# The opening of a two-model kernel: decay's second low-rank product behind the first value chunk, ScalarE's splits and read-outs ahead of mixes, the key factor spread inside r's first chunk

## The chip, the cores and the metric

The kernel runs on one core of a Trainium2 chip. Its time is the device time of one execution in microseconds (us): 1493.51 us as the median of three runs (1492.37 to 1494.57). The core has five engines that follow their own instruction streams and meet at semaphores: TensorE (PE; its weight loads are listed as PEld), VectorE (DVE), ScalarE (ACT), GpSimd (POOL) and SyncE (SP), which here only issues DMAs.

## The reference

Two small models run one after the other on one sequence of 256 tokens with 1024 features. All that the change touches lies in the first 115 us, in the opening of the first layer, an RWKV-7 time mix:

```
x_prev = jnp.pad(h[:, :-1], ((0, 0), (1, 0), (0, 0)))
xx = x_prev - h
xs = h[None] + xx[None] * mu[:, None, None, :]
x_r, x_w, x_k, x_v, x_a, x_g = xs[0], xs[1], xs[2], xs[3], xs[4], xs[5]
rkv = jnp.einsum('pbtd,pde->pbte', jnp.stack([x_r, x_k, x_v]), w_rkv)
w = -jax.nn.softplus(-(w0 + jnp.tanh(x_w @ w1) @ w2)) - 0.5
decay = jnp.exp(-jnp.exp(w.astype(f32)))
a = jax.nn.sigmoid(a0 + (x_a @ a1) @ a2)
g = jax.nn.sigmoid(x_g @ g1) @ g2
kk = to_heads((k * k_k).astype(f32))
kk = kk / jnp.maximum(jnp.linalg.norm(kk, axis=-1, keepdims=True), 1e-12)
k = k * (1.0 + (a - 1.0) * k_a)
...
_, y = lax.scan(step, S0, (tm(r_h), tm(w_h), tm(k_h), tm(v_h), tm(kk), tm(b_h)))
```

Six mixes of each token with the one before feed three large products (k, v, r, each 1024 x 1024) and three low-rank pairs: decay (64), rate a (64) and gate (160). The keys are normalised for each of 16 heads. The scan over tokens then needs all of it. Behind it come the layer's output, an MLP, attention, and the second model, which the change leaves as they are.

## The kernel before, in words

**Large products.** A weight matrix comes in units of 128 x 2048 floats (1 MB). SP loads a unit into one of four `raw` buffers, ScalarE rounds it to `whi` (`hi_unit`, L418, two buffers), VectorE takes the remainder `wlo = raw - whi` (`lo_unit`, L874, two buffers), and TensorE makes three passes for each product: hi x hi, hi x lo, lo x hi (`passes`, L1631 to L1633). The inputs are split likewise into `XH` and `XL`. A chunk is two units: 512 output columns in two PSUM banks. The chunks of the opening are k0, k1 (units 0 to 3), v0, v1 (4 to 7) and r0, r1 (8 to 11). Chunks take the banks 0, 1 and 2, 3 in turn. The split of unit u needs unit u - 2 to be used up (`unit_used`), and its load needs unit u - 4 to be split (`lo_done`).

**What sets the order.** Each engine's stream is written out by hand and runs strictly in that order; `hi_upto(n)` and `lo_upto(n)` put the splits of all units below n at that place. A wait of one instruction holds everything behind it on its engine.

**The opening's side work.** The input is normalised and turned into `hT`. VectorE makes the mixes: `mix(1)` for w, `mix(2)` for v, `mix(3)` for a, `mix(4)` for r, `mix(5)` for g (L1085, eight instructions each); those that feed large products are split by ScalarE (`mix_to_hi`, L608) and VectorE (`mix_to_lo`, L1095). ScalarE also copies chunks out of PSUM (`read_chunk`: k by L487, v by L491).

- `decay_and_rate` (L1830): first products of decay and rate, after k1. ScalarE's tanh and copy follow (L617).
- `gate_in` (L1838, L1840): first products of the gate, after v0, into banks 6 and 7; ScalarE's sigmoids follow (L624, L626).
- `head_sums` (L1748): sums of squared keys per head, bank 0; VectorE reads them (`head_means`, L1021), ScalarE takes the root (`head_roots`, L565), VectorE inverts (`head_inverses`, L1028, L1029), TensorE spreads the factor to all features (`head_spread`, L1764), VectorE multiplies (L1157).
- The second low-rank products (L1866) first for decay, then for rate, in banks 4 to 7, between `head_sums` and v1; ScalarE's sigmoids follow (L634), then for decay a scaling to `lwT` (L641). VectorE's running sum over tokens (the scan, L1142) waits for it, and `centred` (L1150) closes that block.
- `gates` (L1880, L1884): second products of the gate, in the middle of r0.
- At the end VectorE makes the scan's operands (L1167 to L1172, the semaphore `prepared`), and TensorE's `prepare(0)` (L1911, L1920) starts the blockwise inverse, whose first step on VectorE is L1189.

Of the kernel before, what the change touches and what calls it, by code (L numbers as in the profile page):

```python
# [166 lines left out]
def build(nc, a, out):  # L167

    with ExitStack() as ctx:
# [191 lines left out]
        def _(sp):  # L361
# [26 lines left out]
            for name, kt, nn in GEMMS:  # L388
                if kt:
                    for i in range(nn * kt // UK):  # L390
# [20 lines left out]
        def _(act):  # L411
# [217 lines left out]

            for q, (dst, bias) in enumerate(((sT, "w0"), (aT, "a0"))):  # L630
# [6 lines left out]
                if q == 0:  # L637

                    act.wait_ge(lora2_read, 4)
                    act.wait_ge(mix_lo, 2)  # L640
                    act.activation(lwT, sT, ACT.Copy, scale=-float(np.exp(-0.5))).then_inc(lw_ready, 1)  # L641
# [1667 lines left out]
```

## Time and profile before

| what | us |
|---|---|
| median of three runs | 1493.51 (1492.37 to 1494.57) |
| the profiled execution's own time | 1492.59 |
| its span, first to last instruction | 1490.7 |
| TensorE busy | 1413.4 (95%) |
| VectorE busy | 938.7 (63%) |
| ScalarE busy | 704.6 (47%) |
| GpSimd busy | 69.2 (5%) |
| mean granted TensorE clock | 0.986 of full |

The span leaves out some 1.9 us around the first and the last instruction. A busy share is a mean over stages with different limits; TensorE is busy 95% of the whole, but less in the opening, and for a change there only the opening's rows count.

### The profile page before, as it was taken

The numbers are of one execution on the slowest core, as the hardware profiler recorded it, in microseconds if no ns is written. First come the engines' busy times: TensorE is split into PE (matmuls) and PEld (weight loads), VectorE is DVE, ScalarE is ACT, GpSimd is POOL, SyncE is SP. The second block draws the span as 40 slices with busy tenths as digits, with TensorE's granted clock in tenths as the row PEclk, the third lists the DMA queues.
The fourth block names the chain that finished last, engine by engine and source line by source line (L and its number), as shares of the span: only waits on it lengthen the run. The fifth ranks groups of instructions, "written<-read, shape, count | busy, mean of one in ns | idle before, by whom it ended". The sixth has DMA issues, their size and how long they took to land.

```text
span 1490.7 us, 22267 instructions
## 1 busy us (share of the span) xinstructions
PE 1413.4 (95%) x9462; PEld 1213.4 (81%) x9462; DVE 938.7 (63%) x1286; ACT 704.6 (47%) x998; POOL 69.2 (5%) x62
## 2 busy tenths in 40 slices
PE   5889988999999989999999999999999999899998
PEld 5769887888889957888889887778888897688887
DVE  6677675565666586656667643566566577575565
ACT  5473332454445555545444444445444525455443
POOL 0005260000001000000000000000000000000000
PEclk9999999999999999999999999999999999999999
DMA  8320002455555421555575553345555543345552
GB/s 312 111 102 3 30 3 81 168 179 195 198 184 204 170 87 40 187 193 183 191 242 173 198 190 124 136 150 190 197 185 185 202 145 138 113 142 197 192 183 78
DMA packets 35284, 230.42 MB, mean 155 GB/s; under 512 B 4192, under 2 KB 5536, under 8 KB 8560
## 3 DMA queue, kind: packets, MB, share of 16 engines
q1 hardware_dynamic: 33376, 223.43, 43.4%
q0 software_dynamic: 1808, 5.56, 1.2%
q8 instruction: 75, 1.23, 0.3%
q14 instruction: 25, 0.20, 0.0%
HBM read 227.90 MB, written 1.05 MB: 154 GB/s over the span
## 4 chain that ended last, share of the span: by engine, by line
PE 83%; DVE 10%; ACT 5%; issue 2%; DMA 0%; SPq 0%; DVEq 0%; POOL 0%; ACTq 0%
PE bank L1631 16%; PE bank L1632 16%; PE bank L1633 16%; PE bank L1707 15%; PE bank L1710 8%; DVE wlo L874 3%; ACT whi L418 2%; PE bank L1950 2%; PE bank L1593 1%; DVE arena L1085 1%; DVE arena L1204 1%; PE bank L1967 1%; DVE arena L1360 1%; DVE arena L1339 1%; ACT arena L576 1%
## 5 line engine op out<-in xcount | busy, mean ns | idle before, releaser
L874 DVE TENSOR_TENSOR wlo<-raw,whi 128x2048 fp32r<-128x2048 f32 x208 | 478.1, 2299 | 395.4 <-ACT whi L418 395.0
L418 ACT ACTIVATE whi<-raw 128x2048 fp32r<-128x2048 f32 x208 | 398.4, 1916 | 411.8 <-PE bank L1633 276.7
L1631 PE MATMUL bank<-whi,XHL 128*128 128x512 f32 x896 | 352.6, 394 | 11.6 <-DVE XHL L921 7.5
L1632 PE MATMUL bank<-wlo,XHL 128*128 128x512 f32 x896 | 349.9, 391 | 0.0
L1633 PE MATMUL bank<-whi,XHL 128*128 128x512 f32 x896 | 349.6, 390 | 0.0
L1707 PE MATMUL bank<-XHL,whi 128*128 128x512 f32 x1024 | 323.4, 397 | 2.3 <-DVE arena L949 2.2
L1710 PEld LDWEIGHTS bank<-XHL,wlo 128*128 128x128 f32 x1024 | 192.9, 188 | 45.5
L1631 PEld LDWEIGHTS bank<-whi,XHL 128*128 128x128 f32 x896 | 168.7, 188 | 50.6 <-issue 8.1
L1710 PE MATMUL bank<-XHL,wlo 128*128 128x256 f32 x1024 | 201.7, 278 | 0.0
L1633 PEld LDWEIGHTS bank<-whi,XHL 128*128 128x128 f32 x896 | 168.9, 188 | 35.9
L1632 PEld LDWEIGHTS bank<-wlo,XHL 128*128 128x128 f32 x896 | 169.0, 189 | 33.2
L1707 PEld LDWEIGHTS bank<-XHL,whi 128*128 128x128 f32 x1024 | 158.5, 190 | 5.8 <-DVE arena L949 3.0
L1631 PE MATMUL bank<-XHL,whi 128*128 128x256 f32 x512 | 149.3, 292 | 9.1 <-DVE XHL L1100 5.0
L1632 PE MATMUL bank<-XHL,whi 128*128 128x256 f32 x512 | 147.4, 288 | 0.0
L1633 PE MATMUL bank<-XHL,wlo 128*128 128x256 f32 x512 | 147.2, 287 | 0.0
L1631 PEld LDWEIGHTS bank<-XHL,whi 128*128 128x128 f32 x512 | 100.9, 197 | 11.7 <-issue 8.0
L1632 PEld LDWEIGHTS bank<-XHL,whi 128*128 128x128 f32 x512 | 101.1, 197 | 0.1
L1633 PEld LDWEIGHTS bank<-XHL,wlo 128*128 128x128 f32 x512 | 100.9, 197 | 0.0
L508 ACT ACTIVATE arena<-bank 128x256 f32<-128x256 f32 x128 | 47.8, 374 | 49.6 <-PE bank L1710 49.6
L513 ACT ACTIVATE XHL<-arena 128x256 fp32r<-128x256 f32 x128 | 46.1, 410 | 53.1 <-DVE arena L952 53.1
L952 DVE SCALAR_TENSOR_TENSOR arena<-arena 128x256 f32<-128x256 f32 x128 | 54.4, 425 | 4.4
L949 DVE TENSOR_TENSOR arena<-bank,arena 128x256 f32<-128x256 f32 x128 | 53.5, 418 | 0.0
(280 smaller groups left out, 1201.9 us busy)
## 6 DMA issues: line engine op xcount, KB each, us to landing
raw<-in_w_mlp SPq DMA_DIRECT2D x128, 1024.0 KB, 4.8
raw<-in_w_rv SPq DMA_DIRECT2D x8, 1024.0 KB, 5.0
raw<-in_w_rg SPq DMA_DIRECT2D x8, 1024.0 KB, 4.9
raw<-in_w_reo SPq DMA_DIRECT2D x8, 1024.0 KB, 4.8
raw<-in_w_k SPq DMA_DIRECT2D x4, 1024.0 KB, 9.3
raw<-in_w_v SPq DMA_DIRECT2D x4, 1024.0 KB, 5.7
raw<-in_w_r SPq DMA_DIRECT2D x4, 1024.0 KB, 4.8
raw<-in_w_rwo SPq DMA_DIRECT2D x4, 1024.0 KB, 5.0
```

The costliest lines, as they stand in the source:

```text
L418: act.activation(whi[:, u % SPLIT_RING], raw[:, u % RAW_RING], ACT.Copy).then_inc(hi_done, 1)
L508: act.activation(UPL[:, t % 4], psum[up_bank(t)][:, T:2 * T], ACT.Copy).then_inc(up_low, 1)
L513: act.activation(XH[:, KT + t % 8], HID[:, t % 4], ACT.Copy).then_inc(h_hi, 1)
L874: dve.tensor_tensor(wlo[:, u % SPLIT_RING], raw[:, u % RAW_RING], whi[:, u % SPLIT_RING].bitcast(F32), ALU.subtract).then_inc(lo_done, 1)
L949: dve.tensor_tensor(UPZ[:, t % 2], psum[up_bank(t)][:, 0:T], UPL[:, t % 4], ALU.add)\
L952: dve.scalar_tensor_tensor(HID[:, t % 4], UPZ[:, t % 2], 0.0, UPZ[:, t % 2], ALU.max, ALU.mult)\
L1631: pe.matmul(out_, xh[xs], wh[ws], start=start, stop=False)
L1632: pe.matmul(out_, xh[xs], wl[ws], start=False, stop=False)
L1633: return pe.matmul(out_, xl[xs], wh[ws], start=False, stop=stop_)
L1707: pe.matmul(bank[:, :], whi[:, u % SPLIT_RING, k2 + e, cols], XHL[:, kt + e].rearrange("p h t -> p (h t)"), start=(kt + e == 0), stop=False)
L1710: ins = pe.matmul(bank[:, 0:T], wlo[:, u % SPLIT_RING, k2 + e, cols], XH[:, kt + e], start=False, stop=(kt + e == KT - 1))
L1950: ins = pe.matmul(psum[bank][rows, p * HD:(p + 1) * HD], w[rows, f, p], x[rows, f, p], start=(p == 0), stop=(p == KT - 1))
```

## The change

It moves work on four engines, and adds or removes no arithmetic.

- **Loads.** The weight units 2 and 3 (k1's) are issued ahead of the gate's matrix g1 and all that follows it, and no longer behind the constants.
- **ScalarE and VectorE at the start.** The first pair of turned features is handled ahead of the split of unit 0.
- **Around k1.** ScalarE reads k0 and splits unit 3 ahead of splitting the mix for v; VectorE splits unit 3 ahead of it too. ScalarE splits unit 5 right behind reading k1.
- **Behind v0.** TensorE makes decay's second product first, then `gate_in` (now in banks 0 and 1), `head_sums` (now in bank 2), rate's second product. v1 now also waits until VectorE has read bank 2 (`sums_ms`), and r0 until ScalarE has read banks 0 and 1 (`lora1_act`). ScalarE does decay's sigmoids before the keys' squares and the split of unit 7, and the gate's sigmoids after rate's.
- **VectorE behind v0.** `head_means` comes ahead of the split of unit 7, and the split of unit 8 ahead of `head_inverses`.
- **r0.** `head_spread` moves from ahead of r0 to behind its second of eight feature tiles.

```diff
             load_unit("k", 0, 0)
             load_unit("k", 1, 1)
-            for n, dst in (("w1", w1s), ("a1", a1s), ("g1", g1s)):
+            for n, dst in (("w1", w1s), ("a1", a1s)):
                 sp.dma_start(dst.rearrange("p k n -> p (k n)"), a[n]).then_inc(lora_in, 16)
+            load_unit("k", 2, 2)
+            load_unit("k", 3, 3)
+            sp.dma_start(g1s.rearrange("p k n -> p (k n)"), a["g1"]).then_inc(lora_in, 16)
...
             norm_first()
-            hi_upto(1)
             for b in range(4):
+                if b == 1:
+                    hi_upto(1)
                 act.wait_ge(turned, b + 1)
...
             hi_upto(3)
+            read_chunk("k", 0, by_feature(kT))
+            hi_upto(4)
             mix_to_hi(2, 1)
-            read_chunk("k", 0, by_feature(kT))
             read_chunk("k", 1, by_feature(kT))
+            hi_upto(6)
             act.wait_ge(lora1, 2)
...
             mix_to_hi(4, 0)
             read_chunk("v", 0, by_token_plain(V))
-            act.wait_ge(prepared, 1)
-            head_squares(0, KKR)
-            act.wait_ge(lora1, 3)
-            act.activation(sga, psum[6][:, 0:T], ACT.Sigmoid).then_inc(lora1_act, 1)
...
-            hi_upto(U0["v"] + 4)
...
+            act.wait_ge(mixed, 5)
+            low_rank_out(0, sT, "w0")
+            act.wait_ge(prepared, 1)
+            head_squares(0, KKR)
+            hi_upto(U0["v"] + 4)
+            act.wait_ge(lora1, 3)
+            act.wait_ge(lora2_read, 4)
+            act.wait_ge(mix_lo, 2)
+            act.activation(lwT, sT, ACT.Copy, scale=-float(np.exp(-0.5))).then_inc(lw_ready, 1)
+            low_rank_out(1, aT, "a0")
+            act.activation(sga, psum[0][:, 0:T], ACT.Sigmoid).then_inc(lora1_act, 1)
...
+            hi_upto(U0["r"] + 1)
             head_roots(0)
-            hi_upto(U0["r"] + 1)
...
             mix(2, 3)
+            lo_upto(4)
             mix_to_lo(1, 2, 1)
-            lo_upto(4)
             mix(3, 4)
...
-            lo_upto(8)
             dve.wait_ge(lora2, 4)
             head_means(0, 1.0, 0.0)
+            lo_upto(8)
...
+            lo_upto(9)
             head_inverses(0)
-            lo_upto(9)
...
             chunk("v", 0, "token", 1, ready=lambda b: pe.wait_ge(mix_lo, 1))
-            pe.wait_ge(mixed, 5)
-            gate_in()
-            pe.wait_ge(acc_read["act"], READ_COUNT[CHUNK0["v"]][1])
-            pe.wait_ge(const_in, 16 * (len(CONST_KEEP) - 2))
-            head_sums(0, KKSQ)
...
+            low_rank(0, w2s, tw)
+            pe.wait_ge(mixed, 5)
+            pe.wait_ge(acc_read["act"], READ_COUNT[CHUNK0["v"]][1])
+            gate_in()
+            pe.wait_ge(const_in, 16 * (len(CONST_KEEP) - 2))
+            head_sums(0, KKSQ)
+            low_rank(1, a2s, ta)
+            pe.wait_ge(sums_ms, 1)
             chunk("v", 1, "token", 1)
 
-            pe.wait_ge(lora2_read, 8)
-            head_spread(0, rn)
+            def key_spread():
+
+                pe.wait_ge(lora2_read, 8)
+                head_spread(0, rn)
...
-            chunk("r", 0, "feature", 0, ready=lambda b: pe.wait_ge(mix_lo, 2), mid=(4, gates))
+            pe.wait_ge(lora1_act, 4)
+            chunk("r", 0, "feature", 0, ready=lambda b: pe.wait_ge(mix_lo, 2), mids=((2, key_spread), (4, gates)))
```

ScalarE around k1, before (L418 splits a unit, L608 the mix for v, L487 reads a k chunk):

```order
L418 ACTIVATE whi<-raw 128x2048 [waits unit_used,raw_landed2]
L608 ACTIVATE XHL<-arena 128x8x256 [waits mixed]
L487 ACTIVATE arena<-bank 128x512 [waits unit_used]
L487 ACTIVATE arena<-bank 128x512
L418 ACTIVATE whi<-raw 128x2048 [waits unit_used,raw_landed3]
```

and now, where the same lines are L421, L490 and L612:

```order
L421 ACTIVATE whi<-raw 128x2048 [waits unit_used,raw_landed2]
L490 ACTIVATE arena<-bank 128x512 [waits unit_used]
L490 ACTIVATE arena<-bank 128x512
L421 ACTIVATE whi<-raw 128x2048 [waits unit_used,raw_landed3]
L612 ACTIVATE XHL<-arena 128x8x256 [waits mixed]
```

The split of unit 3 has moved ahead of the wait for the mix.

TensorE between v0 and v1, before (L1838 and L1840 are `gate_in`, L1748 `head_sums`, L1866 the second products of decay and then of rate):

```order
L1838 MATMUL bank6<-arena 128x256 [waits mixed]
L1838 MATMUL bank6<-arena 128x256 x7
L1840 MATMUL bank7<-arena 32x256 x8
L1748 MATMUL bank0<-arena,c_head_window 32x256 [waits sq_ready,const_in,acc_read_act]
L1748 MATMUL bank0<-arena,c_head_window 32x256 x7
L1866 MATMUL bank4<-arena 128x256 [waits lora1_act]
...
L1866 MATMUL bank6<-arena 128x256 [waits lora1_act]
...
L1866 MATMUL bank4<-arena 128x256 [waits lora2_read]
...
L1866 MATMUL bank6<-arena 128x256 [waits lora2_read]
```

and now (L1875 are the second products, L1851 and L1853 `gate_in`, L1761 `head_sums`):

```order
L1875 MATMUL bank4<-arena 128x256 [waits lora1_act]
...
L1875 MATMUL bank6<-arena 128x256 [waits lora1_act]
...
L1851 MATMUL bank0<-arena 128x256 [waits acc_read_act,mixed]
L1851 MATMUL bank0<-arena 128x256 x7
L1853 MATMUL bank1<-arena 32x256 x8
L1761 MATMUL bank2<-arena,c_head_window 32x256 [waits sq_ready,const_in]
L1761 MATMUL bank2<-arena,c_head_window 32x256 x7
L1875 MATMUL bank4<-arena 128x256 [waits lora2_read]
...
L1875 MATMUL bank6<-arena 128x256 [waits lora2_read]
```

Decay's product now stands ahead of the gate's, and rate's behind the head sums.

VectorE behind the keys' product with their factor, before (L874 splits a unit, L1021 is `head_means`, L1142 the scan, L1150 its centring, L1028 and L1029 `head_inverses`, L1157 the product with the spread factor):

```order
L874 TENSOR_TENSOR wlo<-raw,whi 128x2048 [waits hi_done]
L1021 TENSOR_SCALAR arena<-bank0 128x256 [waits sums_ready,lora2]
L1138 MEMSET arena 128x16 [waits lw_ready,mix_lo]
...
L1150 TENSOR_TENSOR arena<-arena,small 128x2064 [waits dve_step]
L1028 TENSOR_SCALAR arena<-arena 128x256 [waits sums_sd]
L1029 RECIPROCAL arena<-arena 128x256 [waits dve_step]
L874 TENSOR_TENSOR wlo<-raw,whi 128x2048 [waits hi_done]
L1157 TENSOR_TENSOR arena<-arena,bank4 128x2x256 [waits rn_spread,lora2]
```

and now (L883, L1030, L1148, L1160, L1037, L1038, L1167 in the same roles):

```order
L1030 TENSOR_SCALAR arena<-bank2 128x256 [waits sums_ready,lora2]
L883 TENSOR_TENSOR wlo<-raw,whi 128x2048 [waits hi_done]
L1148 MEMSET arena 128x16 [waits lw_ready,mix_lo]
...
L1160 TENSOR_TENSOR arena<-arena,small 128x2064 [waits dve_step]
L883 TENSOR_TENSOR wlo<-raw,whi 128x2048 [waits hi_done]
L1037 TENSOR_SCALAR arena<-arena 128x256 [waits sums_sd]
L1038 RECIPROCAL arena<-arena 128x256 [waits dve_step]
L1167 TENSOR_TENSOR arena<-arena,bank4 128x2x256 [waits rn_spread,lora2]
```

Both splits have changed places with their neighbour of the key norm.

## Rows read from the trace of the kernel before

**Rows 1.** The page: the chain that ended last, by engine

```profile
PE 83%; DVE 10%; ACT 5%; issue 2%; DMA 0%; SPq 0%; DVEq 0%; POOL 0%; ACTq 0%
```

**Rows 2.** Busy time by stretch: us, PE, PEld, DVE, ACT, POOL, clock, DMA share, GB/s

```profile
0.00:113.70 113.70, 87.77 (x544) 73.44 (x544) 79.40 (x128) 64.68 (x85) 1.23 (x6) 0.94 0.50 172
25.20:40.10 14.90, 14.83 (x123) 14.63 (x122) 12.89 (x20) 5.96 (x5) 0.00 (x0) 1.00 0.63 232
43.10:49.10 6.00, 5.97 (x28) 5.97 (x29) 6.00 (x11) 0.00 (x0) 0.00 (x0) 0.50 0.50 175
61.10:63.20 2.10, 0.04 (x2) 0.02 (x1) 2.10 (x2) 1.91 (x1) 0.00 (x0) 1.00 0.00 0
196.00:198.00 2.00, 1.78 (x34) 1.78 (x36) 1.38 (x3) 0.31 (x1) 1.29 (x1) 0.50 0.00 0
```

**Rows 3.** Timeline of TensorE where k1's and v0's second units start: start, length, [idle before]

```profile
43.13 0.58 PE L1631 MATMUL bank<-XHL,whi 128*128 128x256 f32 x1 [3.10 <-DVE wlo L874]
...
63.18 0.50 PE L1631 MATMUL bank<-whi,XHL 128*128 128x512 f32 x1 [2.06 <-DVE wlo L874]
```

**Rows 4.** Timeline of ScalarE, 35 to 61 us

```profile
36.06 1.92 ACT L608 ACTIVATE XHL<-arena 128x2048 fp32r<-128x2048 f32 x1 [5.53 <-DVE arena L1085]
37.88 1.07 ACT L487 ACTIVATE arena<-bank 128x512 f32<-128x512 f32 x2
38.83 3.71 ACT L418 ACTIVATE whi<-raw 128x2048 fp32r<-128x2048 f32 x2
...
58.90 1.90 ACT L418 ACTIVATE whi<-raw 128x2048 fp32r<-128x2048 f32 x1
```

**Rows 5.** Timeline of VectorE, 37 to 47 us

```profile
38.01 2.29 DVE L1095 TENSOR_TENSOR XHL<-arena,XHL 128x2048 fp32r<-128x2048 f32 x1 [1.99 <-ACT XHL L608]
40.78 2.29 DVE L874 TENSOR_TENSOR wlo<-raw,whi 128x2048 fp32r<-128x2048 f32 x1 [0.48 <-ACT whi L418]
```

**Rows 6.** Timeline of TensorE from v0's end to v1's start

```profile
68.77 3.62 PE L1838 MATMUL bank<-arena 128*128 128x256 f32 x16
...
77.89 2.00 PE L1866 MATMUL bank<-arena 64*128 64x256 f32 x16 [1.07 <-ACT arena L626]
81.28 1.14 PE L1866 MATMUL bank<-arena 64*128 64x256 f32 x8 [1.39 <-ACT arena L634]
...
83.81 0.50 PE L1631 MATMUL bank<-whi,XHL 128*128 128x512 f32 x1
```

**Rows 7.** Timeline of ScalarE, 79 to 85 us

```profile
79.68 3.01 ACT L634 ACTIVATE arena<-bank,vecs 128x256 f32<-128x256 f32 x8
82.72 1.91 ACT L641 ACTIVATE arena<-arena 128x2048 f32<-128x2048 f32 x1
```

**Rows 8.** Timeline of VectorE, 79 to 117 us

```profile
84.78 0.07 DVE L1138 MEMSET arena<- 128x16 f32 x1 [2.35 <-ACT arena L641]
...
97.19 2.47 DVE L1157 TENSOR_TENSOR arena<-arena,bank 128x512 f32<-128x512 f32 x4
99.82 2.29 DVE L874 TENSOR_TENSOR wlo<-raw,whi 128x2048 fp32r<-128x2048 f32 x1 [0.16 <-ACT whi L418]
102.03 2.19 DVE L1167 TENSOR_SCALAR arena<-arena,vecs 128x256 f32<-128x256 f32 x8
...
113.19 2.28 DVE L874 TENSOR_TENSOR wlo<-raw,whi 128x2048 fp32r<-128x2048 f32 x1
115.39 1.28 DVE L1189 TENSOR_TENSOR arena<-bank,c_scan_masks 128x512 f32<-128x512 f32 x2
```

**Rows 9.** Timeline of TensorE from v1's end to the blockwise inverse

```profile
95.23 1.15 PE L1764 MATMUL bank<-arena 32*128 32x256 f32 x16 [0.21 <-issue]
97.38 0.35 PE L1631 MATMUL bank<-XHL,whi 128*128 128x256 f32 x1 [1.00 <-issue]
...
107.80 0.39 PE L1631 MATMUL bank<-XHL,whi 128*128 128x256 f32 x1
...
113.74 2.09 PE L1911 MATMUL bank<-arena 64*64 64x64 f32 x128
```

**Rows 10.** Busy time by stretch, around the end of k0

```profile
32.00:34.00 2.00, 2.00 (x19) 2.00 (x19) 2.00 (x5) 0.00 (x0) 0.00 (x0) 1.00 0.36 53
```

More of the change, by code:

```diff
@@ L620, in _, with low_rank_out @@
             read_chunk("v", 0, by_token_plain(V))
-            act.wait_ge(prepared, 1)
-            head_squares(0, KKR)
-            act.wait_ge(lora1, 3)
-            act.activation(sga, psum[6][:, 0:T], ACT.Sigmoid).then_inc(lora1_act, 1)
-            for b in range(4):
-                ins = act.activation(sgb[b * QUARTER:(b + 1) * QUARTER, :], psum[7][0:QUARTER, 0:T], ACT.Sigmoid)
-            ins.then_inc(lora1_act, 1)
-            hi_upto(U0["v"] + 4)
-            for q, (dst, bias) in enumerate(((sT, "w0"), (aT, "a0"))):
+            def low_rank_out(q, dst, bias):
                 for b in range(4):
@@ L636, in _ @@
                     ins.then_inc(lora2_read, 1)
[L637 to L641, printed above, removed]
+            act.wait_ge(mixed, 5)
[9 more added lines that the diff above has]
+            act.activation(sga, psum[0][:, 0:T], ACT.Sigmoid).then_inc(lora1_act, 1)
+            for b in range(4):
+                ins = act.activation(sgb[b * QUARTER:(b + 1) * QUARTER, :], psum[1][0:QUARTER, 0:T], ACT.Sigmoid)
+            ins.then_inc(lora1_act, 1)
+            hi_upto(U0["r"] + 1)
             head_roots(0)
-            hi_upto(U0["r"] + 1)
             act.wait_ge(centred, 1)
@@ L1017, in head_means @@
             def head_means(i, scale, eps):
-                r, bank = (rn, 0) if i == 0 else (frn, 4)
+                r, bank = (rn, 2) if i == 0 else (frn, 4)
                 dve.wait_ge(sums_ready, i + 1)
@@ L1078, in _ @@
             norm_first()
-            lo_upto(1)
             def mix_tiles(order, mu, ks):
@@ L1108, in _ @@
                 mix_tiles(0, 2, range(2 * b, 2 * b + 2)).then_inc(first_mixed, 1)
-                if b >= 1:
+                if b == 0:
+                    lo_upto(1)
+                else:
                     first_to_lo(b - 1)
@@ L1633, in passes, with chunk @@
                 return pe.matmul(out_, xl[xs], wh[ws], start=False, stop=stop_)
-            def chunk(name, n, form, half=0, kts=KT, ready=None, mid=None, by_rows=False):
+            def chunk(name, n, form, half=0, kts=KT, ready=None, mid=None, by_rows=False, mids=()):
                 g = CHUNK0[name] + n
@@ L1652, in chunk @@
                             mid[1]()
+                        for first_kt, work in mids:
+                            if kt == first_kt:
+                                work()
                         if by_rows and kg == kts // UK - 1:
@@ L1747, in head_sums @@
                     q, j = p // 4, p % 4
-                    ins = pe.matmul(psum[4 if i else 0][32 * j:32 * j + 32, 0:T], keep["head_window"][:, 14 - 2 * q:46 - 2 * q],
+                    ins = pe.matmul(psum[4 if i else 2][32 * j:32 * j + 32, 0:T], keep["head_window"][:, 14 - 2 * q:46 - 2 * q],
                                     sq[:, p], start=(q == 0), stop=(q == 1 and i == 0))
@@ L1837, in gate_in @@
                 for k in range(KT):
-                    pe.matmul(psum[6][:, 0:T], g1s[:, k, 0:P], XM[1][:, k], start=(k == 0), stop=(k == KT - 1))
+                    pe.matmul(psum[0][:, 0:T], g1s[:, k, 0:P], XM[1][:, k], start=(k == 0), stop=(k == KT - 1))
                 for k in range(KT):
-                    ins = pe.matmul(psum[7][0:QUARTER, 0:T], g1s[:, k, P:GATE], XM[1][:, k], start=(k == 0),
+                    ins = pe.matmul(psum[1][0:QUARTER, 0:T], g1s[:, k, P:GATE], XM[1][:, k], start=(k == 0),
                                     stop=(k == KT - 1))
@@ L1849, in _, with low_rank @@
             chunk("v", 0, "token", 1, ready=lambda b: pe.wait_ge(mix_lo, 1))
[L1850 to L1856 removed]
+            def low_rank(q, w2, t1):
                 for half in range(2):
                     if q == 0:
[L1859 removed]
+                        pe.wait_ge(lora1_act, 2)
                     else:
```

4 lines of the change are left out of this document (1 added, 3 removed).

## The prediction, written before the changed kernel ran

> **What bounds the kernel now.** I read the chain of waits first: 83% of it is TensorE, 10% VectorE, 5% ScalarE [rows 1], so time that TensorE does not spend idle or at the slow clock is time won. The table of stretches then says where such time lies in the part that changes: up to 113.7 us TensorE is busy 87.8 us, and its clock averages 0.94 [rows 2]. The timeline of TensorE in that part names the waits, and those of ScalarE and VectorE say what they wait behind. Last I looked at who is late once those waits are gone. There VectorE shows: from 84.78 to 115.39 it runs with one gap of 0.16 us [rows 8]. It will be the new limit, so TensorE's gain is not the answer by itself.
>
> **Part 1, k1's second unit.** TensorE waits 3.10 us for VectorE's split of unit 3 [rows 3]. ScalarE did the mix at 36.06, read k0, and only at 38.83 began units 3 and 4 [rows 4]; VectorE then split unit 3 from 40.78 to 43.07 [rows 5]. A unit of TensorE takes 5.7 us (v1's two run from 83.81 to 95.23 less 0.21 of idle [rows 6, 9]); with TensorE done with unit 2 at 43.13 - 3.10 = 40.03, k0 was done at 34.3. So now: k0 read 34.3 to 35.35 (1.07), unit 3 rounded to 37.2 (3.71 for two, so 1.86), VectorE, free since its mix ended at 36.06, done at 39.5 (2.29). TensorE asks at 40.0: the wait of 3.10 goes, with 0.5 us to spare. With it goes its aftermath: the clock is 0.50 (1.2 GHz) from 43.1 to 49.1, after an idle of 3.10 us, and 1.00 before [rows 2]. Six us at half speed hold 3.0 us of work, so 3.0 us more are lost; I take 2.85, because 5.97 of the 6.00 was work and the edges are blurred. Sum of part 1: 5.95 us. The mix for v now ends its two splits at 38.9 and 41.7, and v0 wants it at 49.
>
> The Trainium skill, TensorE: Matmul & The Clock Gate, section "HAM oscillation — how this bites in real kernels", says that an idle gap throttles the array again and the slow start is paid anew. The trace agrees at 43.1, and at 61.1 to 63.2, where 2.06 us of idle left the clock at 1.00 [rows 2, 3].
>
> The loads cannot spoil this. The same bytes go out in another order, and at 32 to 34 us the DMA share is down to 0.36 [rows 10], so the whole list including v's first units is nearly drained when k1 starts at 34.3. The start itself (pair 0 ahead of unit 0's split on both engines) only swaps neighbours on one chain; I count 0 to 0.3 us and take 0.
>
> **Part 2, v0's second unit.** The wait of 2.06 us [rows 3] came from ScalarE rounding unit 5 at 58.90 [rows 4], behind tanh and the next mix. Now it stands right behind reading k1, done near 48.7, and VectorE's part near 52.5; TensorE, 5.95 us early, asks at 55.1. The 2.06 goes: 8.0 us ahead at v0's end, 60.75 for 68.77.
>
> **Part 3, between v0 and v1.** Before: 68.77 to 83.81 = 15.04 us with waits of 1.07, 1.39 and 0.32 (81.28 + 1.14 to 82.74) [rows 6]. Now the same products follow each other: decay 2.0 (operands ready at 51.5), gate and head sums 77.89 - 1.07 - 68.77 = 8.05, rate 2.0. Their waits are over: v0 is read at 61.9 while decay's product runs to 62.75, the keys' squares are ready at 68.1, decay's sigmoids (3.01, [rows 7]) end at 66.2. Sum 12.05, v1 starts at 72.8, 11.0 ahead. The added wait for VectorE's read of bank 2 needs head sums (70.8) plus 0.42: 71.3, under rate's product. If it were late, v1 and all behind it would queue.
>
> **Part 4, VectorE's chain.** Its start is decay's `lwT`, which overwrites what `gate_in` reads. ScalarE is free at 69.9 (sigmoids to 66.2, squares to 68.1, unit 7 to 69.9), the gate's first products end at 69.5; 1.91 more [rows 7] gives 71.85. VectorE reads bank 2 at 70.9 to 71.3 and splits unit 7 to 73.5, so its scan starts at 73.55 where it started at 84.78 [rows 8]: 11.2 ahead. From there the same instructions follow, but for one wait. Before, the product with the spread factor started 12.41 after the scan's start (84.78 to 97.19) with no idle. Now this work ends at 73.55 + 12.41 - 0.05 = 85.9 to 86.1, and TensorE spreads only after two tiles of r0. v1 ends at 72.8 + 11.3 = 84.1, half a unit is 2.9, half of the spread (1.15, [rows 9]) gives the first bank at about 87.9. VectorE idles 1.85 us; the old 0.16 goes. So L1189, at 115.39 before, comes 11.2 - 1.85 + 0.16 = 9.5 us earlier, at 105.9.
>
> **Part 5, TensorE up to there.** Before, v1's end to the inverse was 95.23 to 113.74 = 18.5 us with 0.21 and 1.00 of waiting [rows 9]; now 17.3, ending at 101.4, 12.3 ahead. But the rest waits for VectorE: operands at 101.6, r0's read by ScalarE is tied to the last of them (103.75, then 1.07), r1's first tiles to VectorE's split that ends at 105.9 (113.19 + 2.28 before, [rows 8]). What follows is a loop of TensorE, ScalarE, VectorE and GpSimd that starts with those. TensorE's 12.3 is cut to VectorE's 9.5.
>
> **The sum.** Behind the opening nothing is edited and every load waits for a split, not for a clock time, so I expect the 9.5 to stay. The profiled execution took 1492.59 (span 1490.7 and 1.9 around it); less 9.5 is 1483.1. It was 0.9 below the median of three; on the median's footing the forecast is 1493.5 - 9.5 = 1484.0 us. The unseen prices and their bounds: splitting r0 in two for the spread costs between nothing and the 1.2 us of the old seams [rows 9], I take nothing; a missed margin at k1 costs up to 1 us; slow stretches of the clock after gaps in later stages may fall otherwise when everything moves by 9.5. One such shows at 196 to 198, clock 0.50 [rows 2]. The one at 43.1 cost 2.85; for those I allow 2 either way.
>
> **Rivals.**
> 1. *TensorE's figure holds.* If VectorE's chain were not the limit (POOL and ScalarE starting their parts by TensorE's arrival), 12.3 go: 1481.2. For it: TensorE is 83% of the chain. Against: VectorE's row at 115.39 starts the moment its split ends. Chance 0.12.
> 2. *Half a gain: the clock's share is not there.* The page named above also says that the activity monitor's window is free-running, which would make the fall after a short idle a matter of position. By rows: the fall at 43.1 came after 3.10 us, none after 2.06. If the execution profiled was one of few with that fall, the edit saves 9.5 - 2.85 = 6.65: 1486.9. For it: 3.10 and 2.06 are close. The three runs lie within 2.2 us, which can hide it. A wait of 3 us in front of v1 or inside r0 would land there too. Chance 0.18.
> 3. *Hidden anyway.* A later stage that waits for something else takes the gain back: within 0.2%, 1493 to 1491. For it: VectorE and ScalarE are far from idle in the scan. Against: I find no load or constant with a fixed time there. Chance 0.06.
> 4. *Slower: the low-rank loads.* TensorE's in-order wait ahead of k1 asks for all sixteen low-rank loads, which now stand behind 2 MB more. At 232 GB/s (mean of 25.2 to 40.1, [rows 2]) these take 9 us. k1 waits as soon as the last lands after 34.3, and the kernel is slower than before once that is later than 34.3 + 9.5 = 43.8: for example at 47, 3.2 us and a slow restart of 2.85 us more, 1499.5. Against: the share of 0.36 at 32 to 34 us. Chance 0.04.
>
> **How the numbers follow.** The forecast has 0.60, with its own range 1482.0 to 1486.0. Rivals 1 and 2 are on the same side. Cutting at 1480.5 and 1489.5 leaves out rivals 3 and 4 and the tails of the others, some 0.17. This measurement can tell about 0.2% (3 us) from no change. Faster by more than that: 0.60 + 0.12 + 0.18 = 0.90; within: 0.06; slower: 0.04.
>
> **What would show it.** After: no idle of 1 us ahead of k1's and v0's second units, and the clock at 1.00 from some 25 us to the end of the opening; v1 starting near 72.8; VectorE's scan near 73.5, an idle of about 1.9 ahead of its product with the spread factor, and its first inverse step near 105.9. Wrong it would be if TensorE stood in front of k1 (loads), in front of v1 (bank 2), or inside r0 (the spread) for more than 1 us, or if the stage ends 9.5 early and the span does not.

## The result, and the profile after

The changed kernel takes 1485.40 us (median of 6 runs, 1482.72 to 1488.58), beside 1494.04 for the kernel before (6 runs, 1490.45 to 1498.07): a ratio of 0.9939 [0.992, 0.9958], some 9 us less. The forecast was 1484.0. The profiled execution took 1487.26 with a span of 1485.5, so between the two profiled executions only 5.2 us of the 9 show. Where the other four are is the first thing to read.

I split both spans at three events: the first matmul of k0, VectorE's first step of the inverse, and the first matmul of the first model's MLP.

| stretch, us | before | after | difference |
|---|---|---|---|
| start to k0's first matmul | 20.33 | 22.86 | +2.53 |
| k0 to the first inverse step | 95.06 | 85.60 | -9.46 |
| inverse step to the MLP's first matmul | 168.1 | 172.4 | +4.3 |
| from there to the end | 1207.2 | 1204.6 | -2.6 |
| span | 1490.7 | 1485.5 | -5.2 |

The stretch in which the waits lay is 9.46 us shorter; forecast were 9.5. The last two aren't edited. The table of the experiments shows by how much they move from profile to profile, and at which clock.

The places in the opening, in TensorE's timeline of the changed kernel (start, length, idle before):

```profile
22.86 0.55 PE L1641 MATMUL bank<-XHL,whi 128*128 128x256 f32 x1 [4.78 <-DVE XHL L1108]
...
62.56 2.00 PE L1875 MATMUL bank<-arena 64*128 64x256 f32 x16
64.49 3.72 PE L1851 MATMUL bank<-arena 128*128 128x256 f32 x16
...
72.58 2.00 PE L1875 MATMUL bank<-arena 64*128 64x256 f32 x16
74.50 0.50 PE L1641 MATMUL bank<-whi,XHL 128*128 128x512 f32 x1
86.23 0.35 PE L1641 MATMUL bank<-XHL,whi 128*128 128x256 f32 x1 [0.53 <-DVE wlo L883]
89.27 1.15 PE L1777 MATMUL bank<-arena 32*128 32x256 f32 x16
95.23 3.70 PE L1900 MATMUL bank<-arena 128*128 128x512 f32 x8 [1.76 <-DVE wlo L883]
105.89 2.10 PE L1932 MATMUL bank<-arena 64*64 64x64 f32 x128
```

TensorE stands idle no more in front of k1's and v0's second units [rows 3] or between v0 and v1 [rows 6]. All waits of TensorE from 20 to 108 us of the changed kernel are three (us in total, times, longest):

```profile
PE bank L1641 <- DVE XHL L1108: 4.8, 1, 4.8
PE bank L1900 <- DVE wlo L883: 1.8, 1, 1.8
PE bank L1641 <- DVE wlo L883: 0.5, 1, 0.5
```

The first of them is k0's own start; before it was 5.0. The same table of the kernel before, with 5.2 us for k1 and v0 in its first row (two rows of `issue`, 1.2 us, are left out):

```profile
PE bank L1631 <- DVE wlo L874: 5.2, 2, 3.1
PE bank L1631 <- DVE XHL L1100: 5.0, 1, 5.0
PE bank L1866 <- ACT arena L634: 1.7, 2, 1.4
PE bank L1866 <- ACT arena L626: 1.1, 1, 1.1
```

VectorE's timeline after, for [rows 8]; it is the chain that carries the gain on:

```profile
39.32 2.29 DVE L883 TENSOR_TENSOR wlo<-raw,whi 128x2048 fp32r<-128x2048 f32 x1 [0.88 <-ACT whi L421]
...
73.15 2.28 DVE L883 TENSOR_TENSOR wlo<-raw,whi 128x2048 fp32r<-128x2048 f32 x1
75.39 0.07 DVE L1148 MEMSET arena<- 128x16 f32 x1
...
90.50 2.48 DVE L1167 TENSOR_TENSOR arena<-arena,bank 128x512 f32<-128x512 f32 x4 [2.56 <-PE bank L1777]
...
106.26 2.29 DVE L883 TENSOR_TENSOR wlo<-raw,whi 128x2048 fp32r<-128x2048 f32 x1
108.46 1.28 DVE L1199 TENSOR_TENSOR arena<-bank,c_scan_masks 128x512 f32<-128x512 f32 x2
```

The product with the spread factor (L1167) now waits 2.56 us for TensorE, where it had no idle before; behind it VectorE runs without a gap to the inverse. Busy time by stretch after (columns as in [rows 2]), around the old slow stretch and in the unedited stage:

```profile
22.80:26.80 4.00, 3.94 (x18) 3.97 (x19) 3.93 (x10) 2.56 (x3) 0.00 (x0) 1.00 1.06 260
26.80:47.80 21.00, 21.00 (x176) 20.88 (x174) 20.12 (x31) 8.90 (x7) 0.00 (x0) 1.00 0.59 208
108.46:280.90 172.44, 158.26 (x2411) 144.15 (x2407) 106.02 (x190) 54.49 (x97) 52.63 (x37) 0.93 0.13 46
280.90:1485.50 1204.60, 1169.31 (x6364) 997.77 (x6364) 751.64 (x970) 583.68 (x815) 13.66 (x20) 0.99 0.49 168
```

The same two late stretches of the kernel before:

```profile
115.39:283.50 168.11, 152.36 (x2458) 139.37 (x2448) 105.62 (x190) 54.91 (x96) 52.59 (x37) 0.98 0.13 47
283.50:1490.70 1207.20, 1171.57 (x6364) 998.92 (x6364) 751.96 (x970) 583.54 (x815) 13.66 (x20) 0.99 0.49 168
```

From 26.8 to 47.8 TensorE has no idle at all and runs at full clock: the stretch at 0.50 from 43.1 to 49.1 [rows 2] is gone. In the scan's stage the same instructions take 4.3 us more, at a clock of 0.93 where it was 0.98. (The counts differ, 2411 for 2458, because some matmul records are missing.) Behind it the changed kernel has one slow stretch fewer, six for seven.

The late start has its row on ScalarE, which waits for the small table `vecs` before its first squares. Changed kernel:

```profile
9.19 0.63 ACT L437 ACTIVATE arena<-X 128x512 f32<-128x512 f32 x1 [3.88 <-DMA vecs<-in_vecs]
```

The kernel before:

```profile
6.54 0.63 ACT L434 ACTIVATE arena<-X 128x512 f32<-128x512 f32 x1 [1.24 <-DMA vecs<-in_vecs]
```

The table landed 6.6 us after its issue, and 3.9 us before the change. Two theories were open: the new order of the loads delays it, or it is chance.

### The profile page after: what moved, and what is told of

Its sections match the earlier page's. It is cut to its first block, busy times and chain, and to the rows that moved or that the text cites. A ratio compares the mean times of both kernels' runs of the same rounds, so it can differ in the third digit from the quotient of the medians.

```text
span 1485.5 us, 22271 instructions
## 1 busy us (share of the span) xinstructions
PE 1414.5 (95%) x9462; PEld 1214.9 (82%) x9462; DVE 938.6 (63%) x1286; ACT 704.9 (47%) x998; POOL 69.2 (5%) x62
## 4 chain that ended last, share of the span: by engine, by line
PE 86%; DVE 8%; ACT 4%; issue 2%; DMA 0%; SPq 0%; DVEq 0%; ACTq 0%
PE bank L1641 17%; PE bank L1642 16%; PE bank L1643 16%; PE bank L1720 15%; PE bank L1723 8%; DVE wlo L883 2%; PE bank L1971 2%; ACT whi L421 2%; PE bank L1603 1%; PE bank L1988 1%; DVE arena L1214 1%; PE bank L2067 1%; DVE arena L1349 1%; ACT arena L579 1%; PE bank L2101 1%
## 5 line engine op out<-in xcount | busy, mean ns | idle before, releaser
L883 DVE TENSOR_TENSOR wlo<-raw,whi 128x2048 fp32r<-128x2048 f32 x208 | 478.1, 2299 | 376.8 <-ACT whi L421 376.5
L421 ACT ACTIVATE whi<-raw 128x2048 fp32r<-128x2048 f32 x208 | 398.7, 1917 | 412.6 <-PE bank L1643 278.0
L1641 PE MATMUL bank<-XHL,whi 128*128 128x256 f32 x512 | 147.7, 288 | 5.3 <-DVE XHL L1108 4.8
L1642 PE MATMUL bank<-XHL,whi 128*128 128x256 f32 x512 | 145.9, 285 | 0.0
L511 ACT ACTIVATE arena<-bank 128x256 f32<-128x256 f32 x128 | 47.8, 374 | 49.6 <-PE bank L1723 49.6
## 6 DMA issues: line engine op xcount, KB each, us to landing
raw<-in_w_k SPq DMA_DIRECT2D x4, 1024.0 KB, 11.4
```

Of the source, the lines that this page charges most:

```text
L421: act.activation(whi[:, u % SPLIT_RING], raw[:, u % RAW_RING], ACT.Copy).then_inc(hi_done, 1)
L511: act.activation(UPL[:, t % 4], psum[up_bank(t)][:, T:2 * T], ACT.Copy).then_inc(up_low, 1)
L883: dve.tensor_tensor(wlo[:, u % SPLIT_RING], raw[:, u % RAW_RING], whi[:, u % SPLIT_RING].bitcast(F32), ALU.subtract).then_inc(lo_done, 1)
L1641: pe.matmul(out_, xh[xs], wh[ws], start=start, stop=False)
L1642: pe.matmul(out_, xh[xs], wl[ws], start=False, stop=False)
```

## The experiments

Each profile was split at the same events as above. "Step" is the time from k0's first matmul to VectorE's first inverse step. One more piece of chance sits in it: k0 begins with TensorE at half speed (its matmuls of 256 columns start every 0.213 us instead of 0.12), for 3.1 to 6.1 us. "Slow" is that length (to 0.1 us or so); half of it is lost, and "net" is the step less that half. "Scan stage" runs from the step to the MLP.

| kernel | median us (runs) | ratio to before [95%] | k0 starts | slow | step | net | scan stage, clock |
|---|---|---|---|---|---|---|---|
| before (profile) |  |  | 20.33 | 5.0 | 95.06 | 92.5 | 168.1, 0.98 |
| changed | 1485.40 (6) | 0.9939 [0.9920, 0.9958] | 22.86 | 4.0 | 85.60 | 83.6 | 172.4, 0.93 |
| 1 again | 1484.22 (6) | 0.9929 [0.9914, 0.9944] | 20.28 | 3.8 | 85.42 | 83.5 | 172.4, 0.93 |
| 2 loads back | 1485.35 (6) | 0.9935 [0.9919, 0.9951] | 20.19 | 4.0 | 85.56 | 83.6 | 173.1, 0.92 |
| 3 k1 only | 1487.68 (12) | 0.9959 [0.9945, 0.9973] | 21.18 | 3.1 | 91.01 | 89.5 | 170.1, 0.95 |
| 4 k1 undone | 1489.55 (8) | 0.9968 [0.9955, 0.9981] | 21.23 | 6.1 | 91.27 | 88.2 | 172.4, 0.93 |
| 5 spread ahead | 1485.17 (5) | 0.9938 [0.9923, 0.9953] | 20.41 | 4.3 | 85.56 | 83.4 | 170.3, 0.95 |
| 6 spread at tile 1 | 1482.35 (5) | 0.9917 [0.9903, 0.9932] | 20.48 | 3.3 | 84.38 | 82.7 | 167.4, 0.98 |
| 7 and split first | 1482.48 (5) | 0.9921 [0.9904, 0.9938] | 20.28 | 5.0 | 85.12 | 82.6 | 167.9, 0.98 |
| 8 vecs late | 1482.27 (5) | 0.9918 [0.9904, 0.9933] | 19.04 | 5.3 | 86.16 | 83.5 | 167.5, 0.98 |
| 9 k1 and v0 only | 1486.22 (6) | 0.9948 [0.9927, 0.9968] | 20.94 | 6.1 | 87.02 | 84.0 | 170.3, 0.95 |
| 10 tile 1, vecs late | 1480.80 (6) | 0.9916 [0.9897, 0.9934] | 19.04 | 4.0 | 84.63 | 82.6 | 167.6, 0.98 |
| 11 all | 1480.42 (6) | 0.9913 [0.9894, 0.9931] | 19.04 | 5.3 | 84.26 | 81.6 | 169.6, 0.96 |

The kernel before took 1495.51 (19 runs) beside 1 to 4, 1493.46 (9) beside 5 to 8, 1492.68 (11) beside 9 to 11; so ratios are compared across groups, medians only within one.

**1. The changed kernel again.** Nothing edited; it stands beside the same runs of the kernel before as the next three.

> The changed kernel once more, nothing edited. In its first profile the small table of gains (vecs) landed 6.6 us after its issue (3.9 in the kernel before) and the whole start was 2.6 us late. Theory A, chance: this time vecs lands after about 3.9 us, ScalarE's squares begin near 6.5, k0 near 20.2 and VectorE's first inverse step near 105.9; time 9.5 us below before. Theory B, the moved weight loads crowd it out: it lands after 6 us or more again, squares near 9, the first inverse step near 108.5, time 6 to 8 us below before.

Measured: k0 starts at 20.28 and the first squares at 6.61, `vecs` 4.0 us after its issue. The late start of the first profile was that execution's. The step is 85.42, 9.6 shorter than before, and net of the slow start 83.5 beside 92.5: 9.0 shorter. In the first profile it is 8.9.

**2. The order of the loads taken back.**

```diff
-            for n, dst in (("w1", w1s), ("a1", a1s)):
+            for n, dst in (("w1", w1s), ("a1", a1s), ("g1", g1s)):
                 sp.dma_start(dst.rearrange("p k n -> p (k n)"), a[n]).then_inc(lora_in, 16)
-            load_unit("k", 2, 2)
-            load_unit("k", 3, 3)
-            sp.dma_start(g1s.rearrange("p k n -> p (k n)"), a["g1"]).then_inc(lora_in, 16)
...
-                        if u >= 4:
+                        if u >= 2:
```

> The changed kernel with the load order of before (k1's units behind the constants). Theory A (the late start was chance, and k1 never waited for its loads): the same time as the changed kernel within 1 us, k1 without a wait. Theory B (the moved loads crowd vecs out): 2 to 3 us faster than the changed kernel, vecs landing after 3.9 us. A third reading, that the moved loads feed k1: a wait ahead of k1's units, slower by as much.

Measured: 1485.35 beside 1484.22, steps 85.56 and 85.42. The moved loads neither cost nor give anything that shows. With the run before it, the late `vecs` was chance: in twelve of the thirteen profiles here it landed 3.9 to 4.9 us after its issue, under both orders, and the 6.6 of the changed kernel's first profile came once in nine profiles with the new order. Rival 4 has no ground.

**3. Part 1 alone, on the kernel before.**

```diff
             hi_upto(3)
-            mix_to_hi(2, 1)
             read_chunk("k", 0, by_feature(kT))
+            hi_upto(4)
+            mix_to_hi(2, 1)
...
-            mix_to_lo(1, 2, 1)
             lo_upto(4)
+            mix_to_lo(1, 2, 1)
```

> The kernel before with part 1 alone: k0's read and the split of unit 3 ahead of the mix for v. My theory: the idle of 3.10 us and the slow clock behind it go, k1 ends 5.95 us earlier (45.8 for 51.7), and since nothing else has moved, the scan starts and the inverse's first step come 5.5 to 6 us earlier: 1487.5 to 1488 on the 1493.5 footing. Rival (the slow clock there is chance): about 3.1 us earlier in most runs, 1490.5.

Measured by time: a ratio of 0.9959, 6.1 us of 1495.5 (4.0 to 8.2 by the interval), as expected; the rival's 3.1 lies outside. Its profile shows a step of 91.01, 4.05 shorter (3.1 net), not 5.5 to 6. The clock fell behind v0's wait, which has the length it had in [rows 3]. It fell 1.3 us after TensorE had started again, where the spacing of the matmuls goes from 0.23 to 0.43 us:

```profile
57.15 0.50 PE L1632 MATMUL bank<-whi,XHL 128*128 128x512 f32 x1 [2.10 <-DVE wlo L875]
...
58.87 0.63 PE L1632 MATMUL bank<-whi,XHL 128*128 128x512 f32 x1
```

By stretch, there and once more at the end of the low-rank products and the start of v1:

```profile
58.60:62.00 3.40, 3.40 (x10) 2.66 (x9) 3.40 (x6) 0.00 (x0) 0.00 (x0) 0.53 0.67 272
80.00:83.00 3.00, 3.00 (x9) 2.39 (x10) 2.64 (x10) 3.00 (x9) 0.00 (x0) 0.62 0.56 235
```

2.06 us of idle left the clock at 1.00 before the change, and 2.10 us brought it to about half here. That is the mechanism of rival 2: after idle of this length the fall isn't certain. The profile adds up with it: v0 ends 43.19 us behind k0's start instead of 48.44, net 4.3 earlier, which is the 5.95 of the sum less 1.7, half of the first slow stretch (3.4 us). The other 1.2 goes with the second one. It stands behind three waits of 1.02, 1.40 and 0.33 us within 5 us; the kernel before, and run 9, have much the same three, and their clock stayed at 1.00.

**4. Part 1 undone, in the changed kernel.** The opposite edit, with all the rest of the change in place.

```diff
             hi_upto(3)
-            read_chunk("k", 0, by_feature(kT))
-            hi_upto(4)
             mix_to_hi(2, 1)
+            read_chunk("k", 0, by_feature(kT))
...
-            lo_upto(4)
             mix_to_lo(1, 2, 1)
+            lo_upto(4)
```

> The changed kernel with part 1 taken back. My theory: TensorE waits some 3 us for unit 3 and runs at the slow clock behind it, so v0 starts 5.9 us later than in the changed kernel; VectorE's chain is fed by TensorE (v0's end, then the gate's first products), so the first inverse step is 5.9 us later too, and the time 5 to 6 us above the changed kernel. Rival (the slow clock is chance): 3 us above. Rival (VectorE's chain is the limit all along): 0 to 2 us above.

Measured: the wait is back (3.09 for 3.10), and so is a slow stretch:

```profile
44.52 0.58 PE L1640 MATMUL bank<-XHL,whi 128*128 128x256 f32 x1 [3.09 <-DVE wlo L882]
```

```profile
44.50:48.00 3.50, 3.48 (x16) 3.48 (x17) 3.50 (x9) 0.00 (x0) 0.00 (x0) 0.52 0.71 229
```

It lasts 3.4 us where before it was 6.0 [rows 2], so it costs some 1.7 and not 3.0; 3.1 and 1.7 are the 4.8 by which this kernel's net step is longer than that of run 1 (88.2 and 83.5, 4.7). By time, the kernel loses 5.3 us to the changed one of the same comparison (1489.55 beside 1484.22). The 95% interval of that difference, from the single times, is some 3.9 to 7.0. With the 6.1 of run 3, part 1 is worth 5.3 to 6.1 us in either surroundings, beside 5.95 in the sum. Of that 3.1 is the wait, so the clock's share is 2.2 to 3.0 on the average of the runs. Its size is known roughly (0.8 to 5 us by the two intervals), but neither holds nothing, so it isn't a rarity of one profile.

**5. The spread ahead of r0, where it was.**

```diff
+            key_spread()
             pe.wait_ge(lora1_act, 4)
-            chunk("r", 0, "feature", 0, ready=lambda b: pe.wait_ge(mix_lo, 2), mids=((2, key_spread), (4, gates)))
+            chunk("r", 0, "feature", 0, ready=lambda b: pe.wait_ge(mix_lo, 2), mids=((4, gates),))
```

> The changed kernel with the spread of the key factor back ahead of r0. In the changed kernel VectorE idles 2.5 us in front of its product with the spread factor, because TensorE reaches the spread only behind two tiles of r0. Times counted from k0's start. My theory (VectorE's chain is the limit here): TensorE now waits some 2 us for the factor with nothing to do, yet the product comes 1.9 us earlier, and so does all of VectorE's chain, until TensorE's own end of r0 (2 to 3 us later than now) takes over: the first inverse step 1.0 to 1.9 us earlier than in the changed kernel, time 1 to 2 us lower. Rival (TensorE's work is the limit, the spread inside r0 is a gain): the first inverse step 2 us later, time 2 us higher.

Measured: a miss. 1485.17, ratio 0.9938, and a net step of 83.4, beside run 1's 83.5: no gain, and not the rival's loss either. TensorE, which now had nothing of r0 to do while ScalarE took roots, stood 2.34 us, and the clock fell behind it:

```profile
85.67 1.70 PE L1777 MATMUL bank<-arena 32*128 32x256 f32 x16 [2.34 <-issue]
```

```profile
85.60:89.40 3.80, 3.73 (x26) 3.11 (x27) 2.02 (x4) 3.80 (x5) 0.00 (x0) 0.57 0.55 233
```

VectorE got its factor only 0.5 us earlier than in run 1 (66.97 for 67.45 behind k0's start), as the spread itself now took 1.70 us instead of 1.15. TensorE's first product for the inverse came 1.4 us later (84.25 for 82.84), and VectorE's first step waited for it:

```profile
105.97 1.29 DVE L1199 TENSOR_TENSOR arena<-bank,c_scan_masks 128x512 f32<-128x512 f32 x2 [0.54 <-PE bank L1933]
```

So VectorE was freed of a part of its wait, and TensorE turned into the limit by its own idle. This run also measures TensorE's room: here the step started 1.3 us behind the first product, in run 1 2.6 us behind it, so 1.3 us are to spare there.

**6. The spread one tile earlier.** Between the two: behind r0's first tile.

```diff
-            chunk("r", 0, "feature", 0, ready=lambda b: pe.wait_ge(mix_lo, 2), mids=((2, key_spread), (4, gates)))
+            chunk("r", 0, "feature", 0, ready=lambda b: pe.wait_ge(mix_lo, 2), mids=((1, key_spread), (4, gates)))
```

> The spread one tile earlier, behind the first tile of r0. My theory: the factor is ready 0.2 us behind that tile, so TensorE waits hardly, VectorE's product and with it the first inverse step come 1.4 to 1.5 us earlier than in the changed kernel, time 1.5 us lower. Rival (TensorE is the limit): no change.

Measured: the idle ahead of the product is 1.31 instead of 2.56, and the step 84.38, 1.0 shorter (0.8 net). VectorE's next split lost 0.25 to ScalarE:

```profile
86.56 2.48 DVE L1167 TENSOR_TENSOR arena<-arena,bank 128x512 f32<-128x512 f32 x4 [1.31 <-PE bank L1777]
89.29 2.29 DVE L883 TENSOR_TENSOR wlo<-raw,whi 128x2048 fp32r<-128x2048 f32 x1 [0.25 <-ACT whi L421]
```

The inverse's first step follows VectorE's product, and moves with it. TensorE's first product for the inverse moved too, by the same 1.0 us (81.80 for 82.84 behind k0's start), because its wait for the split of unit 9 inside r0 shrank from 1.76 to 0.64. That it wasn't the one to set the step is seen from the step again starting 2.6 us behind it, where 1.3 would do (run 5).

**7. Run 6, and VectorE's split of unit 7 ahead of `head_means` as it was.**

```diff
+            lo_upto(8)
             dve.wait_ge(lora2, 4)
             head_means(0, 1.0, 0.0)
-            lo_upto(8)
```

> As the one before, and VectorE splits unit 7 again ahead of reading the head sums. My theory: the split fills VectorE's idle time in front of the head sums, the scan starts 1.0 us earlier, v1 still finds bank 2 read in time, the first inverse step 2.0 to 2.2 us earlier than in the changed kernel, time 2 us lower. Rival: v1 waits for bank 2 and passes its delay on, so nothing is won over the kernel with the spread moved alone.

Measured: the scan did start 1.2 us earlier than in run 6, net, and v1 wasn't held up by bank 2, yet nothing came of it. VectorE's split behind the product waited for ScalarE:

```profile
86.17 2.48 DVE L1167 TENSOR_TENSOR arena<-arena,bank 128x512 f32<-128x512 f32 x4 [1.45 <-PE bank L1777]
89.83 2.29 DVE L883 TENSOR_TENSOR wlo<-raw,whi 128x2048 fp32r<-128x2048 f32 x1 [1.18 <-ACT whi L421]
```

The idle ahead of the product grew to 1.45 for all that the scan began sooner, and ScalarE's rounding of unit 9, behind its read of v1 and so tied to TensorE, became the wait behind it. Net of the slow start, which was 1.7 us longer than in run 6, the step is 82.6 beside 82.7: VectorE's gain was lost, 0.1 of it to TensorE and 0.9 (1.18 - 0.25) to ScalarE.

**8. ScalarE's wait for `vecs` behind the squares,** which don't use it.

```diff
-            act.wait_ge(vecs_in, 16)
             act.wait_ge(eps_ready, 1)
             norm_first()
+            act.wait_ge(vecs_in, 16)
```

> The changed kernel with ScalarE's wait for the table of gains put behind the first squares and scalings, which don't read it. The profiles so far show the table landing 3.9 to 6.6 us after its issue and the squares starting 6.5 to 9.2 us into the span. My theory: the squares start at 5.3 to 5.8 us, bound by the activation table and by x, everything is 1.2 to 3 us earlier and the spread between runs gets smaller; 2 us lower in the median. Rival (x's last quarter lands as late, or the turned pairs wait for the gains all the same): under 0.7 us.

Measured: the first squares start with the input's landing and the table load's end, and k0 at 19.04, the earliest of all but run 10 and 11, which share the edit:

```profile
5.30 0.63 ACT L437 ACTIVATE arena<-X 128x512 f32<-128x512 f32 x1
```

```profile
19.04 0.55 PE L1641 MATMUL bank<-XHL,whi 128*128 128x256 f32 x1 [4.84 <-DVE XHL L1108]
```

Ratio 0.9918. The wait for the table stands on the path of every execution, and costs 1.2 us where it lands soon, 3.9 where late. The net step is 83.5, as in run 1: in the opening the edit moves the start and nothing else.

**9. Parts 1 and 2 alone, on the kernel before.** The edit of run 3, and:

```diff
             read_chunk("k", 1, by_feature(kT))
+            hi_upto(6)
             act.wait_ge(lora1, 2)
```

> The kernel before with parts 1 and 2 (both waits ahead of second units), the block between v0 and v1, the order behind it, the loads and the spread as before. Counted from k0's start, which takes the chance of the start out (95.1 us to VectorE's first inverse step in the kernel before, 85.4 in the changed one). My theory: parts 1 and 2 give 8.0 of the 9.5 us: 87.0 to 87.5, time 7 to 8 us below before, and all the rest of the change only 1.5 to 2. Rival: the block between v0 and v1 is worth its 3 us or more and parts 1 and 2 some 5 (their slow stretch being chance): 89 to 90.

Measured: a step of 87.02, 8.0 shorter, and 84.0 net: 8.5 of the 8.9 to 9.0 that the whole change has. So all the rest of it, the larger part of its lines, gives 0.4 to 0.5 us in the opening. By time the ratio is 0.9948, 7.8 us, beside 0.9929 to 0.9939; the intervals overlap.

**10. Run 6 and run 8 together.**

> The changed kernel with the spread behind r0's first tile and the wait for the gains put late. Theory: the two gains are in different places and add: first inverse step 84.4 us from k0's start, k0's start near 19.0, time 3.5 to 4 us below the changed kernel (1480 to 1481). Rival (the later stages take it back): no better than either alone, 1482.3.

Measured: k0 at 19.04 and a net step of 82.6, so each edit does beside the other what it did alone. 1480.80, ratio 0.9916. That ratio is no better than the 0.9917 and 0.9918 of each alone; intervals of 0.0018 to either side don't resolve a gain of 1 us.

**11. Run 10 with the split of run 7, and ScalarE's rounding of unit 9 ahead of its read of v1,** which takes away what spoilt run 7.

```diff
+            hi_upto(U0["r"] + 2)
             read_chunk("v", 1, by_token_plain(V))
```

> As the one before, with VectorE's split of unit 7 ahead of the head sums, and ScalarE's split of unit 9 ahead of reading v1. In the run with the earlier split alone, VectorE stood 1.2 us waiting for ScalarE's part of unit 9 and won nothing. Theory: that wait goes and the first inverse step comes 0.9 to 1.0 us earlier still, 83.4 to 83.5 from k0's start, time 1 us below the one before. Rival (another wait takes its place): the same time as the one before.

Measured: step 84.26, and net 81.6, 1.0 shorter than run 10: with ScalarE out of the way the scan's earlier start does count. 1480.42 beside 1480.80 isn't told apart by time. By its opening it is the best version here, though its ratio isn't told apart from those of runs 6 to 8 and 10: 12 us ahead of the kernel before, and 2 to 4 ahead of the changed one by the ratios.

## Why the prediction was right

**What bounds it.** Right for the inverse's first step: TensorE's chain was the place to look, and VectorE's set how much of its gain counts.

**Part 1.** Right in place and size. The split of unit 3 ended at 39.32 + 2.29 = 41.6, and TensorE took the unit at 41.96 without idle, with 0.34 us to spare (forecast 0.5). Runs 3 and 4 put 5.3 to 6.1 us on it, forecast 5.95. The single profile can't give that number: the slow stretch behind one and the same idle of 3.1 us was 6.0 us long in one execution and 3.4 in another.

**Part 2.** Right: 8.0 at v0's end was forecast for parts 1 and 2. v0 ends 62.56 - 22.86 = 39.7 us behind k0's start in the changed kernel and 48.4 in the kernel before, net 8.2 earlier; in run 9 it is net 8.5, there and at the inverse.

**Part 3.** v1 starts 74.50 - 22.86 = 51.6 us behind k0's first matmul, before it was 83.81 - 20.33 = 63.5; net of the two slow starts (4.0 / 2 and 5.0 / 2) it comes 11.3 earlier, forecast 11.0. The wait for bank 2 cost nothing: VectorE read it at 72.81, and rate's product ran until v1's start.

**Part 4.** VectorE's scan starts 75.39 - 22.86 = 52.5 behind k0, before 84.78 - 20.33 = 64.5: net 11.4 earlier, forecast 11.2. Its idle ahead of the product was 2.56, forecast 1.85. Most of these 0.7 is TensorE's 0.53 of waiting at 86.23, for VectorE's own split of unit 8, which the prediction didn't have. So 11.4 - 2.56 + 0.16 = 9.0 net, where 9.5 was forecast; the other 0.5 of the 9.46 that the two profiles differ by is the shorter slow start (1.0 / 2). The hit to the hundredth is luck, and the mis-sized term is this idle.

**Part 5.** Right that TensorE's gain is cut: of part 3's 3.0 us hardly 0.5 was left at the inverse (run 9). But the cut wasn't where the prediction had it, behind a TensorE that is 12.3 ahead. TensorE's first product for the inverse came 105.89 - 22.86 = 83.0 behind k0, before it was 93.4: net 9.9 earlier. Nearly all of the missing 2.4 are its two new waits, 0.53 and 1.76, for VectorE's splits of units 8 and 9, which the prediction let pass without a wait. (Its 17.3 also takes off 0.21 us of idle that lies ahead of the 95.23 it counts from; 17.5 would be right.) The 1.76 did no harm at the inverse, where TensorE has 1.3 us to spare (run 5), but it is over 1 us of standing inside r0, which the prediction had named as a sign of being wrong, there for the spread. And VectorE's own gain at the scan's start, 11.4, shrank to 9.0 by waiting for TensorE's spread behind v1 and two tiles of r0. So the path runs through TensorE up to the spread, and only from there through VectorE. Run 6, with the spread a tile earlier, shows that.

**What was missed.** The start. The prediction took the 20.3 us up to k0 as fixed, where `vecs` scatters it by 2.6 us, and the wait for it was a row one could have read (1.24 us idle, in the kernel before). And the bound of 2 us either way for slow stretches later was too small for a single execution: the scan's stage took 167.4 to 173.1 us over the profiles here, the longer the lower its clock, and what follows it 1204.5 to 1207.2. In the two profiles of the result the opening's step was 9.46 shorter and the span only 5.2. The prediction had named that, too, as a sign of being wrong; here it came from the start and the scan's stage, and run 1, the same kernel, has a span 8.1 shorter. In the ratios over six runs it doesn't show.

**The rivals.** Rival 1 (1481.2, ratio 0.9918) lies outside the first interval but inside the second, so time alone doesn't exclude it. The traces do: TensorE's first product for the inverse came 9.9 earlier and not 12.3, and in run 5, where it came 1.4 later than in run 1, the step moved by 0.1. Rival 2 (1486.9, ratio 0.9956) lies inside the first interval, by its edge, but outside the second, [0.9914, 0.9944], and runs 3 and 4 put more than the bare wait on part 1. Its mechanism is real all the same: a fall of the clock after 2 to 3 us of idle is neither sure nor of a fixed length. The Trainium skill, TensorE: Matmul & The Clock Gate, section "HAM oscillation — how this bites in real kernels", has the slow start paid again after an idle gap. The traces agree in run 3 (2.10 us, the clock fell); at 61.1 to 63.2 of the kernel before, which the prediction counts as agreement too, the clock stayed at 1.00 behind 2.06 us. So for short gaps it is a price with a chance. Rivals 3 and 4 show nowhere.

**What stays open.** Why the scan's stage runs at a clock of 0.98 in some profiles and at 0.93 in others. The kernel before and runs 6, 7, 8 and 10 have 0.98, the changed kernel 0.93 in both its profiles. The edits don't sort them: run 8 has the changed kernel's order but for its start, and has 0.98. What does go with it is the place of the falls. One slow stretch begins about 80 us behind the inverse's first step in every profile: 79.5 to 80.6 us behind it in the five with 0.98, 79.1 to 79.4 in the three with 0.95, 78.7 to 78.9 in the four with 0.92 and 0.93, and 81.5 in run 11 with 0.96. The profiles with 0.98 have one more slow stretch in the stage, the others three more. So shifts of the falls by 1 or 2 us against the stage go with up to 5.7 us of time. The executions of the kernel before also scatter by themselves, from a mean clock of 0.980 to 0.989 over the span and from 1490.4 to 1498.9 us. Whether an edit shifts the stage the same way in every execution isn't known; if so, some of what runs 6 to 8 gained over the changed kernel (1 to 3 us by the ratios, with 0.8 and 1.2 us at their own places) came from there.

## What to carry to other kernels

When a trace has TensorE waiting for a producer, look first at what stands ahead of that producer on its own engine: two moves, each of a split that TensorE needs next ahead of work that is needed later, gave 8.5 of 9 us in the opening. Then compute who is late next, because the gain is that engine's and not the one's that stopped waiting: a wait taken away at one place (runs 5 and 7) came back at the next. And compare two profiles from event to event and net of the slow starts, or chance in the start and in stages that aren't touched is taken for the edit's effect.

## What the runs showed of the hardware

- After much the same idle of TensorE the clock did different things: 2.06 us, no fall; 2.10, a slow stretch of 3.4 us; 2.34, 3.4; 3.09, 3.4; 3.10, 6.0. The spacing of matmuls nearly doubles in each fall. In run 3 TensorE had been running again at full speed for 1.3 us when it came. Three waits of 1.02, 1.40 and 0.33 us within 5 us had a slow stretch behind them in run 3, and none in the kernel before and in run 9.
- The granted clock's column isn't always true. From 22.8 to 26.8 us of the changed kernel it says 1.00, yet the matmuls start every 0.21 us; the kernel before has the same spacing from 20.4 to 25.2 and the column says 0.50. The column shows the slow start in six of the thirteen profiles, where it lasts 5.0 to 6.1 us, and not in the seven others, where it lasts 3.1 to 4.3. From 26.83 on the changed kernel's matmuls start every 0.12 us; before, with start and length:

```profile
24.49 0.41 PE L1642 MATMUL bank<-XHL,whi 128*128 128x256 f32 x1
24.70 0.41 PE L1643 MATMUL bank<-XHL,wlo 128*128 128x256 f32 x1
24.91 0.41 PE L1641 MATMUL bank<-XHL,whi 128*128 128x256 f32 x1
```

- A table of 88 KB, issued among some MB of other loads, lands 3.9 to 4.9 us after its issue in twelve profiles, and 6.6 in one.
